# The second block's projections, gates and three mixers put into one stage

## The reference, cut to what matters

```python
h = rmsnorm(x, norm_w)
a_q, a_f, a_i, a_z, b_x, b_z, c_z, c_xbc, c_dt, gate_logits = split(h @ w_in)
o_a = rmsnorm(hgrn2_mixer(a_q, a_f, a_i), hgrn_norm_w) * silu(a_z)      # 8 heads of 128
o_b = rglru_mixer(b_x, ...) * silu(b_z)                                 # conv of 4 taps, gates, scan
o_c = rmsnorm(ssd_mixer(c_xbc, c_dt, ...) * silu(c_z), ssd_norm_w)      # conv of 4 taps, 16 heads of 64
x = x + sum_n sigmoid(gate_logits[n]) * (o[n] @ w_out[n])
return rmsnorm(x, final_norm_w)
```

## Time and profile before

| what | us |
|---|---|
| median of 3 runs | 5011.13 (5006.65 to 5017.52) |
| profiled execution | 5013.51 |
| its span, first to last instruction | 5011.7 |
| TensorE busy in the span | 4459.3 (89%) |
| VectorE busy | 2839.6 (57%) |
| ScalarE busy | 1805.9 (36%) |
| GpSimd busy | 47.5 (1%) |

### The profile page before, as it was taken

One profiled execution on the slowest core, in us unless ns is written; L12 is line 12 of the kernel. 1 busy time (PEld: TensorE's weight loads), 2 busy tenths in 40 slices (PEclk: granted clock), 3 DMA queues, 4 the chain that ended last, 5 costly groups with the idle time before them and its releaser, 6 DMA issues. The chain is left out here.

```text
span 5011.7 us, 78264 instructions
## 1 busy us (share of the span) xinstructions
PE 4459.3 (89%) x29238; PEld 3883.0 (77%) x29238; DVE 2839.6 (57%) x4736; ACT 1805.9 (36%) x2603; POOL 47.5 (1%) x63
## 2 busy tenths in 40 slices
PE   9799999998989968899999999999987997439986
PEld 1694445878988858799999997888866997329985
DVE  0449774775783454447766655555554445674445
ACT  0430001434733323344445544444443443324432
POOL 0000000000000000000000000000000000200000
PEclk9899999989999989899999999999998998679998
DMA  7356553347763314456655556666643543004542
GB/s 307 118 191 238 225 226 117 132 152 265 271 211 98 95 42 155 153 179 203 205 187 175 177 183 214 216 215 214 214 164 119 183 171 119 9 1 168 180 172 101
DMA packets 229478, 847.73 MB, mean 169 GB/s; under 512 B 86368, under 2 KB 124608, under 8 KB 139968
## 3 DMA queue, kind: packets, MB, share of 16 engines
q1 hardware_dynamic: 229312, 845.48, 49.1%
HBM read 794.95 MB, written 50.45 MB: 169 GB/s over the span
## 5 line engine op out<-in xcount | busy, mean ns | idle before, releaser
L282 DVE TENSOR_TENSOR rounded<-arena,rounded 128x1024 fp32r<-128x1024 f32 x696 | 852.0, 1226 | 1036.9 <-ACT rounded L275 1036.9
L275 ACT ACTIVATE rounded<-arena 128x1024 fp32r<-128x1024 f32 x696 | 736.3, 1059 | 1178.7 <-PE bank L353 760.4
L351 PE MATMUL bank<-rounded,rounded 128*128 128x256 f32 x3520 | 1008.5, 286 | 130.7 <-DVE rounded L282 130.7
L352 PE MATMUL bank<-rounded,rounded 128*128 128x256 f32 x3520 | 1006.1, 286 | 0.0
L353 PE MATMUL bank<-rounded,rounded 128*128 128x256 f32 x3520 | 1005.7, 286 | 0.0
L351 PEld LDWEIGHTS bank<-rounded,rounded 128*128 128x128 f32 x3520 | 685.5, 195 | 135.1 <-DVE rounded L282 135.1
L352 PEld LDWEIGHTS bank<-rounded,rounded 128*128 128x128 f32 x3520 | 685.5, 195 | 0.0
L353 PEld LDWEIGHTS bank<-rounded,rounded 128*128 128x128 f32 x3520 | 684.8, 195 | 0.0
L2018 PE MATMUL bank<-rounded,rounded 128*128 128x256 f32 x2048 | 590.8, 288 | 2.7 <-DVE rounded L2143 2.7
L2020 PE MATMUL bank<-rounded,rounded 128*128 128x256 f32 x2048 | 579.8, 283 | 0.0
L2019 PE MATMUL bank<-rounded,rounded 128*128 128x256 f32 x2048 | 579.7, 283 | 0.0
(11 more groups left out here) (358 smaller groups left out, 6374.5 us busy)
## 6 DMA issues: line engine op xcount, KB each, us to landing
arena<-in_w_in SPq DMA_DIRECT2D x244, 1024.0 KB, 4.9
arena<-in_peer_u SPq DMA_DIRECT2D x128, 1024.0 KB, 5.2
arena<-in_peer_v SPq DMA_DIRECT2D x128, 1024.0 KB, 4.9
arena<-in_w_mod SPq DMA_DIRECT2D x96, 1024.0 KB, 6.9
arena<-in_w_out SPq DMA_DIRECT2D x40, 1024.0 KB, 4.9
arena<-in_w_conv_out SPq DMA_DIRECT2D x16, 1024.0 KB, 5.0
arena<-in_w_dn_out SPq DMA_DIRECT2D x16, 1024.0 KB, 4.9
arena<-in_peer_w_q SPq DMA_DIRECT2D x16, 1024.0 KB, 4.9
```

The source lines that it names most:

```text
L275: act.activation(k.staged(0, b), k.raw(r % 2)[:, c], ACT.Copy).then_inc(k.hi_done, 1)
L282: dve.tensor_tensor(k.staged(1, q), k.raw(r % 2)[:, c], k.staged(0, q), ALU.subtract).then_inc(k.lo_done, 1)
L351: pe.matmul(out, wh, hi(kt), start=fresh, stop=False)
L352: pe.matmul(out, wh, lo(kt), start=False, stop=False)
```

## The change

One function `mixers` replaces all stages from "in2" to "gates2", and the three `split` stages. The order of the projection tiles becomes f, b_x, q, i, xbc, z of a, b and c, gates (the weights are laid out so by the host). All 116 tiles are written out half by half, 232 halves, numbered i. On each engine the side steps stand behind the half's own step in a hand-written place:

```diff
-        linear3(k, "in2", w2[0:44], 44, rounded(32), rounded(48), "scalar", keep(64, 44), w2[44:46])
-        linear3(k, "in2z", w2[44:68], 24, rounded(32), rounded(48), "scalar", keep(108, 24, ACT.Silu), w2[68:70])
-        hgrn_decays(k, 64, 132, 140, 148)
-        hgrn_attention(k, 72, 80, 140, 148, 64, 156)
...
-        causal_conv(k, "rg_conv", 88, 132, 8, k.col("rg_cw"), k.col("rg_cb"), False)
-        rglru(k, 132, 116, 88, 140)
-        causal_conv(k, "ssd_conv", 96, 132, 12, k.col("ssd_cw"), k.col("ssd_cb"), True)
-        ssd(k, 132, 124, 96, 144)
...
-        linear3(k, "gates2", w2[68:116], 48, rounded(32), rounded(48), "scalar", keep(132, 48, ACT.Sigmoid), wo2[0:2])
+        mixers(k, w2, rounded(32), rounded(48), wo2[0:2])
...
-            split(k, f"split_b{b}", slot, 108 + 8 * b, slot, 8)
...
+    LEVEL = lambda l: 70 + 6 * l
+    HEAD = lambda h: 140 + 2 * h
...
+        @block.sync
+        def _(sp):
+            for j in range(2, tiles):
+                if j == 6:
+                    sp.dma_start(wa, k.i["rg_wa"]).then_inc(rgw_in, 16)
+                    sp.dma_start(wx, k.i["rg_wx"]).then_inc(rgw_in, 16)
+                if j == 14:
+                    sp.wait_ge(dt_v, 3)
+                    sp.dma_start(incl, k.i["cst"][:, 256 + 14 * P:256 + 15 * P]).then_inc(incl_in, 16)
+                if j == 36:
+                    sp.wait_ge(rg_h, 8)
+                    sp.dma_start(flat(k.t(188, 4))[:, 0:7 * P], k.i["cst"][:, 256:256 + 7 * P]).then_inc(masks_in, 16)
...
+            for i in range(halves):
...
+                mm.then_inc(k.half_done, 1)
+                if i == 20:
+                    dt_turn()
+                if i == 28:
+                    cum()
+                if i in (30, 33, 36, 39):
+                    rg_gates((i - 30) // 3)
+                if i == 67:
+                    v_turn()
+                if i == 70:
+                    score(0, 0)
+                    score(0, 1)
+                for l in range(7):
+                    for c in range(2):
+                        if i == LEVEL(l) + 4 + c:
+                            score(l + 1, c)
+                if i == LEVEL(7) + 5:
+                    across()
+                if i == 121:
+                    attend(0)
+                if i == 125:
+                    attend(4)
...
+                for h in range(SH):
+                    if i == HEAD(h):
+                        rows(h)
+                    if i == HEAD(h) + 5:
+                        y(h)
...
+            for i in range(halves):
+                high(i // 2, i % 2)
+                if i % 2 and i > 1:
+                    evacuate(i // 2 - 1)
+                if i in (10, 11, 12, 18, 19, 20):
+                    decay(i // 18, (i - 10) % 8)
+                if i in (16, 24):
+                    key_exp(i // 24)
+                if i == 14:
+                    dt_small()
+                if i == 15:
+                    dt_small2()
...
+                if 48 <= i < 56:
+                    rg_inverse(i - 48)
...
+                for l in range(8):
+                    for c in range(2):
+                        if i == LEVEL(l) + c:
+                            level(l, c, 0)
+                        if i == LEVEL(l) + 2 + 3 * c:
+                            mask(l, c)
+                        if i == LEVEL(l) + 3 + c:
+                            level(l, c, 1)
...
+                for h in range(SH):
+                    if i == HEAD(h) + 2:
+                        row_diffs(h)
+                    if i == HEAD(h) + 4:
+                        lm_(h)
+                    if i == HEAD(h) + 7:
+                        y_kept(h)
```

More of the change, by code:

```diff
@@ L2447, in _ @@
             act.copy(k.dt_raw[0:H, :], k.ps[0][0:H, 0:L]).then_inc(kept, 1)
-def hgrn_decays(k, f_slot, work, key_slot, sum_slot):
-    nc = k.nc
-    f, t1, key, total = (flat(k.t(s, 8)) for s in (f_slot, work, key_slot, sum_slot))
-    with ExitStack() as stage:
-        a_step, v_step, ones_set = (k.sem(stage, f"hgrn_decay_{n}") for n in ("act", "dve", "ones"))
-        block = stage.enter_context(nc.Block())
-        one = flat(k.t(199, 1))
+F_AT, BX_AT, Q_AT, I_AT, XBC_AT, ZA_AT, BZ_AT, CZ_AT = 64, 72, 80, 88, 96, 108, 116, 124
@@ L2464, in _ @@
             pool.memset(one, 1.0).then_inc(ones_set, 1)
[L2466 to L2485, removed]
@@ new lines, in decay, with scans @@
+            def decay(c, step):
+                f, t1, ky = wide(fs, c), wide(t1s, c), wide(keys, c)
+                if step == 0:
+                    dve.wait_ge(dec_a, 3 * c + 3)
+                    dve.scalar_tensor_tensor(out=t1, in0=f, scalar=0.0, in1=t1, op0=ALU.min, op1=ALU.subtract).then_inc(dec_v, 1)
+                elif step == 1:
+                    dve.wait_ge(dec_v, 2 * c + 1)
+                    dve.tensor_tensor(ky, t1, f, ALU.subtract).then_inc(dec_v, 1)
+            def scans(c, m):
+                dve.wait_ge(ones_set, 1)
+                for h in range(4 * c + 2 * m, 4 * c + 2 * m + 2):
+                    dve.tensor_tensor_scan(tile(sums, h), one, tile(t1s, h), 0.0, ALU.mult, ALU.add).then_inc(scanned, 1)
@@ new lines, in rg_ratio, with rg_input, rg_scan @@
+            def rg_ratio(c):
+                dve.wait_ge(rg_r, 2 + 4 * (c + 1))
+                dve.tensor_tensor(wide(ths, c), wide(ths, c), wide(xr, c), ALU.mult).then_inc(rg_th, 1)
+            def rg_input(c):
+                dve.wait_ge(rg_root, c + 1)
+                dve.tensor_tensor(wide(igs, c), wide(igs, c), wide(ths, c), ALU.mult).then_inc(rg_u, 1)
+            def rg_scan(first):
+                dve.wait_ge(rg_a, 16)
+                for h in range(first, first + 2):
+                    dve.wait_ge(rg_u, h // 4 + 1)
+                    dve.tensor_tensor_scan(tile(ths, h), tile(as_, h), tile(igs, h), 0.0, ALU.mult, ALU.add).then_inc(rg_h, 1)
@@ L2876, in program @@
+    k.raws += tiles
+    k.evacs += tiles
 def program(nc, inputs, out):
```

903 lines of the change are left out of this document (562 added, 341 removed).

## The result

The changed kernel takes 4771.9 us, median of 4 runs (4767.33 to 4775.23), beside 5014.3 us (5006.65 to 5023.29) for the kernel before on the same chip. The ratio is 0.9515, 95% interval 0.9497 to 0.9534: 242 us or 4.8% faster. The forecast was 4769. The profiled execution took 4772.0 us with a span of 4770.2 us, against the 4770.7 us that the prediction's sum gives for a profiled execution.

The account below looks back on a forecast made before the run. Dependent steps bound the mixers' 303 us, TensorE the tiles on both sides. 5013.5 - 326.8 removed + 76.0 products + 8.0 stalls = 4770.7, less 2.4 to the median, gave 4769 us; range 4758 to 4802.

Parts of the forecast that it names:

- (a): Gap from in2 to in2z, beyond the 2.88 us a half costs anyway: 5.7 us removed.
- (b): Gap from in2z to gates2, with all seven mixer and norm stages and TensorE's restart at lower clock: 308.6 us removed.
- (c): Splits ahead of the products out0 to out2: 4.2, 4.2 and 4.1 us, together 12.5 us removed.
- TensorE's products: The mixers' products between halves in TensorE's stream count in full at the warm price: 76.0 us added.
- GpSimd's adds: In seven attention levels adds hold VectorE's operations back and TensorE waits 0.6 us each: 4.1 us added.
- Table loads: ScalarE's function changes in 12 halves; only halves 14 to 16 make TensorE wait: 1.5 us with the odd 0.1.
- Rival 2: Late halves are not taken back, each of 12 table loads costs its full 1.28 us plus: 4783 us; chance 0.08.
- DMA: The recurrence's weights go out between two tile loads and make one load late: 1.0 us added.
- Rest: The end of the larger stage and waits that were missed: 1.4 us added.
- rival 1: Waits add up over 232 halves as in the delta stage, 38 us for 8: 4799 us; chance 0.20 with part-way cases.
- Rival 3: TensorE's clock falls to 1.2 GHz, each half costs 2.4 us more: 5326 us, slower than before; chance 0.02.
- rival 4: A wait holds the mixers in order behind the tiles; only two restarts and the splits go: 4987 us; chance 0.02.

Follow-up runs that it names:

- e4: The changed kernel with the three splits ahead of out0 to out2 as stages of their own again; median 4781.3 us.
- e1: The changed kernel with each attention level's products on VectorE moved ahead of its maskings; median 4764.7 us, ratio 0.9496.
- e2: The changed kernel with GpSimd's 28 adds cut from 512 to 4 columns; whole execution 4773.7 us.
- e6: The changed kernel with the small steps of dt and lambda moved to halves with their function family loaded; dt write-out to first rounding 7.53 us, before 8.85.
- e10: The changed kernel with 31 more table loads, one in each of halves 143 to 174; third rounding to last write-out 748.60 us against 748.81.
- experiment 5: Function-family runs e6, e10 and e11 on the changed kernel; in e6, write-out to third rounding is 15.4 to 15.5 us, with the early load 16.2 to 16.6.
- e11: The changed kernel with 31 more table loads, both of a head in its odd half; third rounding to last write-out 749.77 us against 748.81.
- e5: The changed kernel with each reciprocal of halves 48 to 55 computed twice; third rounding to last write-out 760.50 us, +11.7.

## Why the prediction was right, point by point

The time lay 2.9 us above the forecast, 1.3 us by the profiled executions. The mechanism held: the mixers' 303 us went beside the tiles, and only TensorE's products and a few short stalls stayed. That the sum came so close is partly luck, a cancelling of small terms. Three slips of arithmetic or counting are in the prediction, each without weight: 7 x 0.6 is 4.2 and not 4.1, 4768.3 rounds to 4768, and the table loads stand in 14 halves of the stage, not 12.

- **Removed, 326.8 us.** (a) and (b) can only be read as a whole, since the stages are gone; nothing of them came back. (c) was put back in e4 and costs 12.5 us, as said. One assumption in (c) was off: I let the passage into out0 last 0.66 us as in the earlier trace rows, and it is 1.52, +0.9. In return the restarts of out0 to out2 are shorter: 7.1 us from first to third rounding where the restart in the earlier trace rows had 7.96 (luck again: out0 takes 7.96 in e1, e2 and e6), and the part from out0's first rounding to the end took 2.0 us less than I had carried over.
- **TensorE's products, 76.0 us.** The distances in the stage less 2.88 us come to the counts times the prices: 1.78 for a score call of 8, 0.66 for a head's rows, 0.65 for its state output, 75.9 in all. Doubling the scores gave 28.6 us for 28.2.
- **GpSimd's adds, 4.1 us.** Measured 4.55, in the seven halves named. The mechanism was right, each place was 0.05 larger.
- **Table loads, 1.5 us.** Mis-sized in both parts. The halves 14 to 18 have 0.89 us, near the 1.0. But I took a load standing alone as taken back by the next half, and it costs about 0.28 where a wide operation stands behind it: near halves 20, 24, 48, 60 and 197 the stage has 0.3 to 0.6 us each, 1.9 in all. Together about 2.7. Rival 2's full price is excluded by these and by e10. The 2.7 us that the Trainium skill (ScalarE: Activation LUTs, section "Table sets: the hidden batching unit") gives for a change is more than any took here: from the end of the step before a load to the start of the one behind it is 1.31 us, and in most places 0 to 0.3 us of it is paid.
- **A load that I overlooked, 1.0 us.** The Exp for the decay's constant stands ahead of the first rounding with a table load of 1.28 us, where nothing covers it: 8.85 us from the dt write-out to the first rounding, in place of 7.46. Of these 1.4 us, 0.4 come back before the third rounding, as fewer matmuls then run at the lower clock (experiment 5). The diff shows the load, had I asked of each added instruction whether it stands before the first half.
- **DMA, 1.0 us.** No rounding waits where the recurrence's weights arrive: 0. Two places, near halves 120 and 210, have 0.2 us each that belong to no step that I could name: both are absent in e6, the second also in e4, e10 and e11, so its cause stays open.
- **Reciprocals, 0 to 0.1.** 0, and e5 shows how near they were: the second one is paid at once.
- **Rest, 1.4 us.** This term had no row behind it; with the 1.0 for DMA it made room for the terms of the loads, which were too small.
- **The clock.** 1.00 from 3820 us to the end of the stage, also in e5. **The waits.** 3.3 us in nine places, seven of them 21 us and more apart beside an add, two beside table loads; rival 1 would have had them everywhere. Rival 3 (clock) and rival 4 (order kept) have nothing in the trace.

In sum: stalls in the stage 7.6 us for 8.0; around it +1.0, +0.9 and -2.0; and the part ahead of the stage ended 2.2 us later than in the execution that I started from, which is the run-to-run variation of that part. These come to +1.7 us, where 1.3 was measured.

## What to carry to other kernels

When TensorE's stream is the bound and its neighbours are half idle, dependent chains can be laid beside it almost free. Price them half by half, engine by engine: what exceeds the half's own length is paid nearly in full (a second reciprocal 1.47 of 1.65 us), what fits costs nothing, and a half that TensorE's own products make longer takes in more (31 table loads for 0 us). Then look for what the sum over an engine doesn't show: operations that alternate with another engine's, the first instruction of the stage, and large transfers in the queue between two small ones. A restart of the pipeline was the next thing to go here: 5.1 us each, of which 1.5 are the lower clock behind the pause.

## What the runs showed of the hardware beyond what I expected

A wait of TensorE costs more than the row of waits says. Around the start of half 80 in the changed kernel the last matmul before the wait and the first ones after it are:

```profile
4065.16 0.28 PE L2703 MATMUL bank<-rounded,rounded 128*128 128x256 f32 x1
4065.84 0.36 PE L2701 MATMUL bank<-rounded,rounded 128*128 128x256 f32 x1 [0.40 <-DVE rounded L2932]
4066.03 0.28 PE L2702 MATMUL bank<-rounded,rounded 128*128 128x256 f32 x1
```

The idle time is given as 0.40 us, from the modelled end of a matmul at 4065.44. But the next one would have started 0.12 us after 4065.16, so the stream lost 0.56, and another 0.07 as the first matmul after the pause holds the next one back for 0.19 in place of 0.12: 0.63 us, just what half 81's distance has too much. In e5 it is 1.47 us for waits of 1.2. Starts, not waits, give the price of a stall, and short ones are undercounted most: the nine waits of 3.3 us in the row cost 5.4 by the starts.
